# Expert loop of a two-layer mixture-of-experts kernel: the down half of an expert moved behind the gate and up half of the next

## Time and profile before

| | us |
|---|---|
| median of 3 runs | 2135.91 (2132.34 to 2136.14) |
| the profiled execution's own time | 2130.9 |
| its span, first to last instruction | 2129.2 |
| busy in the span: PE / DVE / ACT / POOL | 1703.2 / 691.4 / 447.2 / 241.1 |
| expert stage of layer 0, first weight request to end of the last down product | 530.8 to 1087.1 |
| expert stage of layer 1, the same | 1551.9 to 2083.9 |
| mean granted clock of TensorE, share of full speed | 0.913 |

### The profile page before, as it was taken

One profiled execution on the slowest core, in us unless ns is written; L12 is line 12 of the kernel. 1 busy time (PEld: TensorE's weight loads), 2 busy tenths in 40 slices (PEclk: granted clock), 3 DMA queues, 4 the chain that ended last, 5 costly groups with the idle time before them and its releaser, 6 DMA issues. The chain is left out here.

```text
span 2129.2 us, 25779 instructions
## 1 busy us (share of the span) xinstructions
PE 1703.2 (80%) x9072; PEld 893.8 (42%) x9073; DVE 691.4 (32%) x1256; ACT 447.2 (21%) x821; POOL 241.1 (11%) x342
## 2 busy tenths in 40 slices
PE   5999999798599789998626999999947689855651
PEld 3444444645344334444315436555524344433330
DVE  2405574733311111111133447775432101211114
ACT  3103333201011111111125115553101101111112
POOL 1002530311100000000020200000111000100001
PEclk9999999898699999999867999999959999987885
DMA  9776844400999999999972002001089999999994
GB/s 367 266 262 208 275 141 149 151 30 34 380 386 358 408 419 405 421 410 397 413 298 106 0 1 89 1 1 33 30 332 392 410 420 406 407 411 411 415 419 158
DMA packets 98212, 565.43 MB, mean 266 GB/s; under 512 B 15908, under 2 KB 34048, under 8 KB 58584
## 3 DMA queue, kind: packets, MB, share of 16 engines
q1 hardware_dynamic: 85104, 522.39, 62.2%
q0 software_dynamic: 7744, 26.22, 3.5%
q10 hardware_dynamic: 5288, 15.80, 1.9%
HBM read 522.88 MB, written 41.50 MB: 265 GB/s over the span
## 5 line engine op out<-in xcount | busy, mean ns | idle before, releaser
L2067 PE MATMUL exp_gps<-moew_wg,all_hT 128*64 128x512 f32 (+1 forms) x480 | 239.7, 624 | 34.5 <-DMA moew_wu<-in_moe_w_up 32.3
L2061 PE MATMUL exp_gps<-moew_wg,all_hT 128*32 128x256 f32 x1088 | 162.8, 465 | 100.0 <-DMA moew_wu<-in_moe_w_up 95.1
L2068 PE MATMUL exp_ups<-moew_wu,all_hT 128*64 128x512 f32 (+1 forms) x480 | 237.5, 619 | 0.0
L587 PE MATMUL abp_ps<-ab_w,all_hT 128*128 128x512 f32 x384 | 169.6, 597 | 0.6 <-PE abp_ps L591 0.3
L2061 PE MATMUL exp_ups<-moew_wu,all_hT 128*32 128x256 f32 x1088 | 162.9, 466 | 0.8 <-issue 0.8
L2061 PEld LDWEIGHTS exp_gps<-moew_wg,all_hT 128*32 128x32 f32 x1088 | 81.4, 133 | 178.0 <-issue 136.3
L2067 PEld LDWEIGHTS exp_gps<-moew_wg,all_hT 128*64 128x64 f32 (+1 forms) x480 | 78.1, 167 | 169.1 <-issue 169.1
L2192 DVE TENSOR_TENSOR all_hT<-all_hT,exp_ups 64x512 f32<-64x512 f32 (+1 forms) x30 | 20.7, 690 | 343.9 <-ACT all_hT L2139 343.9
L2095 PE MATMUL exp_yps<-moew_wd,all_hT 128*64 128x512 f32 (+1 forms) x240 | 115.6, 598 | 20.3 <-issue 20.3
L2097 PE MATMUL exp_yps<-moew_wd,all_hT 128*64 128x512 f32 (+1 forms) x240 | 115.1, 596 | 0.0
L587 PEld LDWEIGHTS abp_ps<-ab_w,all_hT 128*128 128x128 f32 x384 | 71.7, 190 | 98.3 <-issue 96.6
(11 more groups left out here) (408 smaller groups left out, 2483.5 us busy)
## 6 DMA issues: line engine op xcount, KB each, us to landing
moew_wg<-in_moe_w_gate SPq DMA_DIRECT2D x64, 2048.0 KB, 26.6
moew_wu<-in_moe_w_up SPq DMA_DIRECT2D x64, 2048.0 KB, 32.6
moew_wd<-in_moe_w_down SPq DMA_DIRECT2D x64, 2048.0 KB, 31.8
all_X<-in_ada_w SPq DMA_DIRECT2D x40, 1024.0 KB, 7.9
ab_w<-in_ab_w_in SPq DMA_DIRECT2D x6, 2048.0 KB, 8.9
ys<-abp_zero SPq DMA_DIRECT2D x32, 384.0 KB, 8.3
ys<-exp_y ACTq DMA_DIRECT2D x13, 512.0 KB, 8.3
ab_rows<-in_ada_w SPq DMA_DIRECT2D x6, 1024.0 KB, 15.2
```

The source lines that it names most:

```text
L587: last = nc.tensor.matmul(ps[i % RB][:], hT[:, kk, what * P:(what + 1) * P], w[n % S][:, kk, :], start=(kk == 0), stop=(kk == KD - 1))
L2061: last = nc.tensor.matmul(bank[lo + j * Q:lo + (j + 1) * Q, 0:HC], x[:, k, 0:Q], wt[:, k, j * HC:(j + 1) * HC], start=(k == 0), stop=(k == ...
L2067: nc.tensor.matmul(gps[0:rows, :], x[:, k, 0:rows], w.g[q][:, k, :], start=(k == 0), stop=(k == KD - 1))
L2068: last = nc.tensor.matmul(ups[at:at + rows, :], x[:, k, 0:rows], w.u[q][:, k, :], start=(k == 0), stop=(k == KD - 1))
```

## The change

TensorE's order becomes up(n), token transposes of n+1, down(n-1), transposes of h(n). The first expert has no down before it (`first`), and the last down stands alone at the end (`last`). ACT and DVE are put into the same order: silu(n), token copy, copy of y(n-1); and h(n), token copy, copy of y(n-1), hT(n). `up`, `h_transposes` and `down` are now three pieces, each with its own branch on the number of rows (`sized`), where there were two. SP requests gate and up of n+4, then down of n+3: gate 3, gate 4, down 3, gate 5, down 4, ... where it was gate 3, down 3, gate 4, down 4. POOL's part, the slots, the tiles and every matmul, copy and transfer are the same.

```diff
+        def staggered(eng, first, turn, last):
+            rows = rows_of(eng, 0)
+            first(rows)
+            with eng.Fori(0, LOOPS) as i:
+                before = rows_of(eng, i * S)
+                for q in range(1, S + 1):
+                    n = i * S + q
+                    rows = rows_of(eng, n)
+                    turn(n, q % S, i + q // S, (q - 1) % S, i + (q - 1) // S, rows, before)
+                    before = rows
+            before = rows_of(eng, LOOPS * S)
+            for n in range(LOOPS * S + 1, E):
+                rows = rows_of(eng, n)
+                turn(n, n % S, n // S, (n - 1) % S, (n - 1) // S, rows, before, follow=n + 1 < E)
+                before = rows
+            last(E - 1, (E - 1) % S, (E - 1) // S, before)
...
# SyncE
-            def turn(n, q, i):
+            def gate_up(n, q):
                 sp.wait_ge(gu_used, n + 1)
                 load_gate_up(sp, a, layer, w, n + S, q)
+
+            def down(n, q):
                 sp.wait_ge(d_used, n + 1)
                 load_down(sp, a, layer, w, n + S, q)
 
-            with sp.Fori(0, E // S - 1) as i:
+            gate_up(0, 0)
+            AHEAD = (E - S - 1) // S
+            with sp.Fori(0, AHEAD) as i:
                 for q in range(S):
-                    turn(i * S + q, q, i)
-            for n in range((E // S - 1) * S, E - S):
-                turn(n, n % S, n // S)
+                    gate_up(i * S + (q + 1), (q + 1) % S)
+                    down(i * S + q, q)
+            for n in range(AHEAD * S, E - S):
+                if n + 1 < E - S:
+                    gate_up(n + 1, (n + 1) % S)
+                down(n, n % S)
...
# TensorE
+            def h_transposes(n, rows):
+                pe.wait_ge(h_done, n + 2)
+                pe.wait_ge(ht_done, n + 1)
+                ...
+            def down(n, q, i, rows):
+                pe.wait_ge(w.d_ready[q], i * 16 + 16)
+                pe.wait_ge(ht_done, n + 2)
+                pe.wait_ge(y_act, n + 1)
+                pe.wait_ge(y_dve, n + 1)
+                ...
-                rows = pe.value_load(r.cnt[0:1, bass.ds(n, 1)], min_val=0, max_val=TOK)
-                sized(pe, rows, up)
+            def first(rows):
+                up(0, 0, 0, rows)
+                x_transposes(1, 1, 0)
+                h_transposes(0, rows)
+
+            def turn(n, q, i, qb, ib, rows, before, follow=True):
+                up(n, q, i, rows)
                 if follow:
                     x_transposes(n + 1, (q + 1) % S, i + (q + 1) // S)
-                pe.wait_ge(h_done, n + 2)
-                pe.wait_ge(ht_done, n + 1)
-                sized(pe, rows, down)
+                down(n - 1, qb, ib, before)
+                h_transposes(n, rows)
...
# ScalarE
+            def turn(n, q, i, qb, ib, rows, before, follow=True):
+                silu(n, rows)
                 if follow:
                     x_copy(n + 1, (q + 1) % S)
-                sized(act, rows, rows_out)
+                rows_out(n - 1, qb, ib, before)
...
# VectorE
+            def turn(n, q, i, qb, ib, rows, before, follow=True):
+                hidden(n, rows)
                 if follow:
                     x_copy(n + 1, (q + 1) % S)
-                sized(dve, rows, rows_out)
+                rows_out(n - 1, qb, ib, before)
+                turned(n, rows)
```

More of the change, by code:

```diff
@@ L1970, in turns, with rows_of @@
                 turn(n, n % S, n // S)
+        def rows_of(eng, n):
+            return eng.value_load(r.cnt[0:1, bass.ds(n, 1)], min_val=0, max_val=TOK)
         def by_rows(eng, n, work):
-            rows = eng.value_load(r.cnt[0:1, bass.ds(n, 1)], min_val=0, max_val=TOK)
-            sized(eng, rows, work)
+            sized(eng, rows_of(eng, n), work)
+        def staggered(eng, first, turn, last):
[14 more added lines that the diff above has]
+            last(E - 1, (E - 1) % S, (E - 1) // S, before)
         def sized(eng, rows, work):
@@ L2046, in x_transposes, with up, work @@
                 last.then_inc(xtr, 1)
-            def turn(n, q, i, follow=True):
+            def up(n, q, i, rows):
                 x = xT
[L2051 to L2055, removed]
+                pe.wait_ge(w.gu_ready[q], i * 32 + 32)
+                pe.wait_ge(xt_act, n + 2)
+                pe.wait_ge(xt_dve, n + 2)
+                pe.wait_ge(h_done, n + 1)
+                def work(rows):
                     at = 0 if rows == P else H
@@ L2070, in up, with work @@
                     last.then_inc(gu_used, 1)
-                def down(rows):
+                sized(pe, rows, work)
+            def h_transposes(n, rows):
+                pe.wait_ge(h_done, n + 2)
+                pe.wait_ge(ht_done, n + 1)
+                def work(rows):
                     at = 0 if rows == P else H
@@ L2081, in down, with work @@
                     last.then_inc(htr, 1)
[L2082 to L2085, removed]
+                sized(pe, rows, work)
+            def down(n, q, i, rows):
[3 more added lines that the diff above has]
+                pe.wait_ge(y_dve, n + 1)
+                def work(rows):
+                    at = 0 if rows == P else H
                     if rows == Q:
@@ L2099, in down @@
                     last.then_inc(d_used, 1)
-                rows = pe.value_load(r.cnt[0:1, bass.ds(n, 1)], min_val=0, max_val=TOK)
-                sized(pe, rows, up)
+                sized(pe, rows, work)
+            def first(rows):
[4 more added lines that the diff above has]
+                up(n, q, i, rows)
                 if follow:
                     x_transposes(n + 1, (q + 1) % S, i + (q + 1) // S)
-                pe.wait_ge(h_done, n + 2)
-                pe.wait_ge(ht_done, n + 1)
-                sized(pe, rows, down)
+                down(n - 1, qb, ib, before)
+                h_transposes(n, rows)
             x_transposes(0, 0, 0)
[L2110 to L2114, removed]
+            staggered(pe, first, turn, down)
             more.tensor(pe)
@@ L2127, in x_copy, with silu, work @@
                 nc.scalar.copy(xT[:, 0:4, :], xps[0][:]).then_inc(xt_act, 1)
-            def turn(n, q, i, follow=True):
-                rows = act.value_load(r.cnt[0:1, bass.ds(n, 1)], min_val=0, max_val=TOK)
-                def silu(rows):
+            def silu(n, rows):
+                def work(rows):
                     at = 0 if rows == P else H
@@ L2139, in silu, with rows_out, work @@
                     nc.scalar.activation(sg[at:at + rows, :], gps[0:rows, :], ACT.Silu).then_inc(sg_done, 1)
-                def rows_out(rows):
+                sized(act, rows, work)
+            def rows_out(n, q, i, rows):
+                def work(rows):
                     act.wait_ge(d_used, n + 1)
@@ L2151, in rows_out, with first @@
                     act.dma_start(ys[bass.ds(n, 1), 0:rows].rearrange("o p n -> (o p) n"), y[q][0:rows, :]).then_inc(y_free[q], 16)
-                sized(act, rows, silu)
+                sized(act, rows, work)
+            def first(rows):
+                silu(0, rows)
+                x_copy(1, 1)
+            def turn(n, q, i, qb, ib, rows, before, follow=True):
+                silu(n, rows)
                 if follow:
                     x_copy(n + 1, (q + 1) % S)
-                sized(act, rows, rows_out)
+                rows_out(n - 1, qb, ib, before)
             x_copy(0, 0)
[L2159 to L2163, removed]
+            staggered(act, first, turn, rows_out)
             more.scalar(act)
@@ L2180, in x_copy, with hidden, work @@
                 nc.vector.tensor_copy(xT[:, 4:8, :], xps[1][:]).then_inc(xt_dve, 1)
-            def turn(n, q, i, follow=True):
-                rows = dve.value_load(r.cnt[0:1, bass.ds(n, 1)], min_val=0, max_val=TOK)
-                def hidden(rows):
+            def hidden(n, rows):
+                def work(rows):
                     at = 0 if rows == P else H
@@ L2193, in hidden, with turned, work @@
                                             ALU.mult).then_inc(h_done, 1)
-                def rows_out(rows):
-                    at = 0 if rows == P else H
+                sized(dve, rows, work)
+            def turned(n, rows):
+                def work(rows):
                     dve.wait_ge(htr, n + 1)
@@ L2209, in rows_out, with first @@
                     nc.vector.tensor_copy(y[q][0:rows, 512:1024], yps[1][at:at + rows, :]).then_inc(y_dve, 1)
-                sized(dve, rows, hidden)
+                sized(dve, rows, work)
+            def first(rows):
+                hidden(0, rows)
+                x_copy(1, 1)
+                turned(0, rows)
+            def turn(n, q, i, qb, ib, rows, before, follow=True):
+                hidden(n, rows)
                 if follow:
                     x_copy(n + 1, (q + 1) % S)
-                sized(dve, rows, rows_out)
+                rows_out(n - 1, qb, ib, before)
+                turned(n, rows)
             x_copy(0, 0)
[L2217 to L2221, removed]
```

(1 more changed line is left out.)

## The result

The changed kernel takes 2120.98 us (median of 5 runs, 2120.49 to 2123.47) against 2135.91 (5 runs of that comparison, 2132.3 to 2138.53). The ratio is 0.9937, 95% interval 0.9919 to 0.9954. That is 14.9 us less where 8.0 were forecast. The profiled executions stand closer together: the changed kernel's own time in its profile is 2121.0 (span 2119.2) against 2130.9 (span 2129.2), 9.9 us.

What follows compares the result with a forecast made beforehand. The queue of weights was taken to bound both layers' expert stages. Gains of 3.9 us (gap at 640) and 4.1 (stage ends), other terms 0, sum to 8.0: from 2135.9 to 2127.9 us, range 2119 to 2137.

Steps and rivals of the forecast that it cites:

- The waits inside a turn: TensorE's waits for h and its copy, 14.7 us over 778 to 988, vanish but shorten nothing: counted 0.
- the wait before expert 28: Sign for the removed turn waits: TensorE's 8.57 us wait for weights before this expert would grow.
- The gap at 640: Layer 0's queue ran dry at 635 to 645, losing 4.7 us; gate 6 requested near 632 gains 3.9.
- one more branch: TensorE's and DVE's turns get three sections by rows instead of two: 0.1 us each, 0.3 before gate 6, elsewhere 0.
- the prediction's own list: Wrong if a full DMA piece before 1080 falls well, layer 0 down waits exceed 1 us a turn, or new sections stall.
- The ends: In both layers only down 31's product remains after its matrix lands: gain 4.1 us, bounds 0.5 and 4.3.
- within 0.3: Sign for the stage ends: the last down product starts within 0.3 us of down 31's landing in both layers.
- SP, the slots, the stores: Moved requests stand behind no later event, slots still hold three experts ahead, stores and gathers cost nothing: 0.
- A: Queue dries up elsewhere in the first ten experts, by as much as gained at 640; only ends gain: 2131.8, chance 0.20.
- B: Last products run at half clock and the gap stays: 0.5 us gained, 2135.4, chance 0.08.
- C: Each TensorE turn stalls at the added branch section; slower from about 2.5 us a turn, up to 2163; chance 0.07.
- more gain than forecast: Case of a shorter wait in both layers' beginnings: 2120 us, chance 0.05.

Runs made afterwards that it cites:

- engines alone: Against the changed kernel, SP keeps its old request order; only TensorE, ACT and DVE are staggered. Ratio to the kernel before 0.9995, 2134.11 us.
- requests alone: Against the changed kernel, TensorE, ACT and DVE go back to the old order; only SP has the new one. Ratio to the kernel before 1.0100, 2155.7 us.
- layer 1 alone: The changed order in layer 1's experts only, layer 0 as in the kernel before. Ratio to the kernel before 0.9977, 2129.9 us.
- count later: The changed kernel with expert n-1's row count read behind up(n) and the token transposes, not at the loop head. Ratio to the kernel before 0.9942, 2121.38 us.
- third expert early: The changed kernel with expert 2's matrices requested without SP's wait for the first gather. Ratio to the kernel before 0.9980, 2130.47 us.
- both of these: The changed kernel with the late row-count read and the early request of expert 2's matrices together. Ratio to the kernel before 0.9966, 2127.93 us.

## Why the prediction was right, and where its sizes were off

**The bound.** Right. The queue of weights sets both stages: with the new order of the engines alone TensorE loses its waits for h and hT, and the time is the same (0.9995).

**The waits inside a turn.** Right. TensorE's waits in 778 to 988, against the earlier trace rows:
```profile
PE exp_gps L2087 <- DMA moew_wu<-in_moe_w_up: 1.6, 1, 1.6
PE exp_yps L2128 <- DMA moew_wd<-in_moe_w_down: 1.5, 1, 1.5
```
The 14.7 us of waits for h and hT are gone. In part they came back as waits for weights. Over 530 to 1085:
```profile
PE exp_gps L2087 <- DMA moew_wu<-in_moe_w_up: 35.2, 7, 9.4
PE exp_gps L2093 <- DMA moew_wu<-in_moe_w_up: 20.9, 5, 7.8
```
Together these are 56.1 us in twelve waits; before, the same two groups had 35.2 us in seven. Counting this step at 0 was correct. One sign named for it did not come: the wait before expert 28 was to grow from 8.57 and is 7.54 (at 1021.18). The waits stand earlier instead, 9.43 us at 989.42 and 5.34 at 1004.58.

**The gap at 640.** The mechanism was right: gate 6 went out at 634.26 (forecast 632.4), and the shares from 635 to 645 are 1.00 and 1.01. Its size was too large. The four traces of the old order lose 4.7 to 5.1 us in that place; the forecast allowed 0.8 for gate 5, and the three of the new order lose 2.3 to 2.4 at 610 to 625. That leaves 2.5 us net where 3.9 were forecast. Up(1) began at 590.98 instead of 588.9: the loop's head, priced at 0.1 us as one more branch, costs 2.2 with its two reads of a count. By the prediction's own list this is a sign of being wrong: a piece that had been full (0.98) fell to 0.52.

Nevertheless layer 0's queue became 5.5 us shorter on the means. One more account of it is its length less the times of all packets, summed and divided by the sixteen engines: 8.4 us before (7.8 to 9.3), 5.2 after (5.1 to 5.4), 3.1 less. This is not quite the time in which nothing moved, for packets overlap: in layer 1 the same subtraction gives -2.0 and -3.0. So closing gaps gave 2.5 to 3.1 us, and the rest of the 5.5 came from what the forecast did not have.

**The rest of the queue, in both layers.** This is the part that the forecast missed. Layer 1's queue was put at 0, since its DMA share is 1.00 throughout, and it gained 3.8 us on the means. There was no dry place to close; the same bytes went through at 408 GB/s instead of 406, with a share of 1.00 in the one and 1.01 in the other. What changed is how long the packets of the weights take, 17,920 of them in each layer (us, packet times of that queue summed and divided by sixteen):

| | old order of the engines | new order of the engines |
|---|---|---|
| layer 0 | 494.5, 492.2, 493.3, 493.4; requests alone 495.9; layer 1 alone 494.3 | 491.0, 490.5, 490.9; count later 491.3; engines alone 491.0; third expert early 491.2; both of these 490.9 |
| layer 1 | 493.5, 493.0, 495.2, 494.7; requests alone 495.7 | 492.2, 490.5, 491.7; count later 491.3; layer 1 alone 491.6; engines alone 490.3; third expert early 491.8; both of these 491.7 |
| layer 1, whole queue | 528.8, 527.9, 530.3, 529.8; requests alone 529.4 | 526.1, 524.5, 525.7; count later 525.6; layer 1 alone 525.3; engines alone 524.7; both of these 525.7 |

In no row do the two columns meet, though they part by 0.8 to 1.8 us and one column's values spread by up to 3.7. The columns part by the order of the engines, not by that of the requests, to which the expectation for the kernel before, run again, had put it. So in layer 0 the queue's 5.5 us are 3.1 by the subtraction above and 2.5 of quicker packets, less 0.1 for gathers and stores; in layer 1 the packets give 2.6 of the 3.8 and the subtraction 1.1. Why the same transfers pass more quickly when TensorE, ACT and DVE work in the new order, was not isolated. Gathers take 1.3 us less in layer 1 (20.2 to 18.9) and stores 1.4 more (16.7 to 18.2), so the traffic beside the weights falls differently; that this is the cause is a guess.

**The ends.** The mechanism was right in both layers, and the size was 4.1 and measured 2.3 + 1.1 = 3.4 on the means. Two things lie in it. The last product starts 0.56 us behind the landing in every trace of the changed kernel, so the sign "within 0.3" was missed. The forecast had 0.2 for this delay in both layers together, and it is 1.1; by the first traces the starts gained 2.4 + 0.7 = 3.1. On the means they gained 2.6 + 1.4 = 4.0, since the old order's other traces start later than the first (up to 3.7 and 2.6 behind the landing): that this meets the 4.1 is luck. And the product itself lasts longer, 2.70 and 3.05 us on the means instead of 2.33 and 2.73, which takes 0.7 back. That is the clock below full speed, of which the forecast's lower bound spoke and its sum did not. TensorE has just waited 2.75 us in layer 0's end. Over all versions in the new order the eight products at a lower clock stand behind waits of 2.05 to 3.23 us, and the seven at the full clock behind waits of 1.49 to 1.96. But in the old order four of eleven lose the clock behind a wait of 0.43. That the wait now standing ahead of the product lowers its clock is therefore not shown.

**SP, the slots, the stores.** In layer 0's first turns no request of the new order stands behind a later event, as forecast. The experiment with the engines alone shows what was not said: the new order of requests is as necessary as that of the engines.

**Rivals.** A (2131.8) and B (2135.4) fall outside what was timed. What A said of the queue was half true: it does dry up again at gate 5, by half of what is gained at 640. C needed stalls of 2.5 us in every turn; in layer 0 TensorE's waits for nothing shown are 2.23 us before up(1), 1.26 before up(7) and 0.43 before up(6), 3.9 in all. The two long ones stand where the loop begins a round of three experts, none at an added section; in layer 1 there are three over 1 us, all before gate products (2.67, 2.23 and 1.53), where the kernel before has one of 3.51. The Trainium skill (Runtime: NRT & Kernel Launch, section "Instruction fetch mechanics") has a taken branch wait for code when its target lies outside the window already fetched. The page of the changed kernel counts the same packets of code as before, and no row shows such a stall:
```profile
q8 instruction: 48, 0.79, 0.2%
q14 instruction: 28, 0.23, 0.0%
```
The prediction read the first of these two lines alone. Together they are 76 packets in either kernel, more than the 64 turns, so "fewer than the turns" does not hold for the whole run. It holds for each stage: 15 and 14 packets before, 16 and 15 after, for 32 turns each.

**Between the stages.** Put at 0 and it lost 1.6 us, in code that the change does not touch. The other versions had 463.3 (the count read later) to 467.4 (requests alone), with no pattern by what was edited. It is open.

**The size of the whole.** The forecast's two mechanisms gave 2.5 to 3.1 and 3.4 us, about 6 of the 8.0 forecast. The rest of the 14.9 comes from parts that the sum did not have. At 2120.98 us it stands beside the last of the prediction's cases, more gain than forecast (2120, given 0.05), and not beside the forecast of 2127.9; and the reason named for that case, shorter waits in both layers' beginnings, is not what the traces show. So the way and the mechanisms are right by reasoning, the nearness of the size is in part luck. Of 14.9 us by the timed runs the traces account for 11: 5.5 + 2.3 + 3.8 + 1.1 - 1.6. The executions that carried a profile took 2130.9, 2131.0, 2133.2 and 2133.3 us for the old order, all below its median, and 2120.8, 2121.0 and 2121.9 for the new. The rest, about 4 us, may lie in the old order's slower executions, of which no trace was caught, unless the 560.5 us of layer 0 in the run with the change in layer 1 alone is one. That stays open as well.

## What to carry to other kernels

When a transfer queue bounds a stage, look for the pieces in which it ran dry and ask which event held back the next request; then move that event, and move the request with it, since either alone can be worth nothing or less (here 0.9995 for the event and 1.0100 for the request, together 0.9937). Put between the last data to land and the end only the work that needs these data. Price what a loop reads at its head: here it was 2.2 us where 0.1 had been counted, ahead of a dry place half as large as the one that was closed; with one read moved away (0.76 us) that place shrank by 0.8. And take more than one trace of each kernel before a difference of a few microseconds is given a cause.

## What the runs showed of the hardware

- Reading one run-time count from on-chip memory on TensorE costs 0.76 us where nothing covers it (2.23 against 1.47 before up(1), 1.26 against 0.51 before up(7)). The load itself takes 0.32 us of that.
- A queue of 6 MB of weights more beside the first gather of tokens delays that gather by 7 us (transposes at 573.62 instead of 566.37).
- The last product, behind a wait for the last weights, lasted 2.5 to 3.6 us instead of 1.93 in five of the six ends of the changed kernel's traces, with a mean granted clock of 0.50 to 0.74. With the other versions in the new order it was three of nine ends, and in the old order four of eleven.
- The same 17,920 packets of weights take 490.5 to 491.3 us in layer 0 with the new order of the engines (sum of their times over sixteen) and 492.2 to 495.9 with the old. At a DMA share of 1.00 to 1.01 over layer 1's queue the engines moved 404 to 409 GB/s; the share alone doesn't tell how fast.
